# Prompt linear and softmax attention placed inside the paged attention of a hybrid decoder step

## The reference, cut to what matters

```
xn = rms_norm(h, norm1);  z = xn @ w_in                # q, k, v of both attentions, gates
S_t = diag(a_t) S_(t-1) + k_t^T v_t;  o_t = q_t S_t      # linear attention, 4 heads, in chunks
p   = softmax(q1 k1^T) - lam * softmax(q2 k2^T)          # differential softmax, 4 heads
o_diff(prompt) = p(causal, over meta + prompt) @ v
o_diff(sample) = p(over cache_k[page_table] and 4 new) @ [cache_v[page_table]; v_new]
h = h + [norm(o_gla) * silu(gate), norm(o_diff) * (1 - lam_init)] @ w_out
h = h + mixture_of_experts(rms_norm(h, norm2))           # top 1 of 4 groups, top 2 of 8 experts
```

## Time and profile before

| | us |
|---|---|
| median of 3 runs | 2400.14 (2399.14 to 2403.88) |
| the profiled execution | 2400.51 |
| its span, first to last instruction | 2398.7 |
| projection | 0 to 355 |
| linear attention, prompt | 355 to 509 |
| linear attention, samples | 509 to 548 |
| softmax attention, prompt | 548 to 778 |
| paged softmax attention | 778 to 1502 |
| merge and routing, experts, combine | 1502 to 2399 |

### The profile page before, as it was taken

How to read it: one execution, slowest core, us unless ns; L and a number is a source line. 1 busy time by engine, 2 the same in 40 slices (tenths; PEclk the granted TensorE clock), 3 DMA queues, 4 the chain that set the end, 5 groups by cost and what they waited for, 6 DMA issues and landing times. The chain is left out here.

```text
span 2398.7 us, 39482 instructions
## 1 busy us (share of the span) xinstructions
PE 2064.1 (86%) x14525; PEld 1516.4 (63%) x14525; DVE 1262.3 (53%) x1975; ACT 1083.9 (45%) x1919; POOL 406.0 (17%) x370
## 2 busy tenths in 40 slices
PE   6999998987887889889888888699179999999991
PEld 5777776765555566565565555255158888888870
DVE  4313414434665534533533533232478888888874
ACT  4312223312443434434434534322067777878760
POOL 0000000000000333233233232000212221212213
PEclk9999999975688999999999999799579999999995
DMA  5121115010000998998998998341079999999976
GB/s 176 49 76 53 64 51 205 1 27 13 1 1 10 392 406 350 404 371 361 392 381 365 380 392 312 133 176 44 10 288 385 404 405 405 404 403 399 407 296 234
DMA packets 106648, 577.14 MB, mean 241 GB/s; under 512 B 14592, under 2 KB 19840, under 8 KB 53520
## 3 DMA queue, kind: packets, MB, share of 16 engines
q0 software_dynamic: 44448, 293.89, 30.6%
q1 hardware_dynamic: 62064, 281.22, 30.3%
HBM read 531.26 MB, written 43.81 MB: 240 GB/s over the span
## 5 line engine op out<-in xcount | busy, mean ns | idle before, releaser
L1792 DVE TENSOR_TENSOR e_l<-first_w,e_h 128x1024 fp32r<-128x1024 f32 x256 | 294.7, 1218 | 10.1 <-ACT e_h L1789 9.9
L1189 PEld LDWEIGHTS ps<-ident,d_ring 128*128 128x128 f32 x2048 | 236.6, 148 | 97.1 <-ACT d_kT L1252 83.6
L1789 ACT CAST e_h<-first_w 128x1024 fp32r<-128x1024 f32 x256 | 250.3, 1049 | 82.3 <-POOLq L1861 42.7
L1252 ACT COPY d_kT<-ps 128x512 f32<-128x512 f32 x256 | 149.8, 586 | 274.7 <-PE ps L1189 272.2
L1189 PE MATMUL ps<-ident,d_ring 128*128 128x128 f32 x2048 | 263.4, 286 | 9.0 <-DMA d_ring<-in_cache_k,d_row 6.9
L1751 PE MATMUL ps<-e_h,e_xh 128*128 128x512 f32 x512 | 207.1, 404 | 3.6 <-DVE e_xl L1801 3.6
L1753 PE MATMUL ps<-e_h,e_xl 128*128 128x512 f32 x512 | 203.9, 398 | 0.0
L1752 PE MATMUL ps<-e_l,e_xh 128*128 128x512 f32 x512 | 203.9, 398 | 0.0
L1300 DVE COPY d_kT<-ps 128x512 f32<-128x512 f32 x256 | 172.4, 687 | 35.6 <-PE ps L1189 31.9
L1238 PE MATMUL ps<-d_ring,d_pT 128*8 128x128 f32 x4096 | 157.8, 280 | 18.2 <-issue 11.8
L304 PE MATMUL ps<-wh,xh 128*128 128x512 f32 (+1 forms) x432 | 173.4, 401 | 0.0
(11 more groups left out here) (321 smaller groups left out, 3513.5 us busy)
## 6 DMA issues: line engine op xcount, KB each, us to landing
first_w<-in_w_down SPq DMA_DIRECT2D x32, 2048.0 KB, 9.0
first_w<-in_w_up SPq DMA_DIRECT2D x62, 1024.0 KB, 8.8
first_w<-in_w_gate SPq DMA_DIRECT2D x62, 1024.0 KB, 11.3
ys_d<-e_y SPq DMA_DIRECT2D x32, 512.0 KB, 10.1
w<-in_w_in SPq DMA_DIRECT2D x6, 2048.0 KB
ys_d<-cat SPq DMA_DIRECT2D x1, 8192.0 KB, 24.7
kT<-in_x_prompt SPq DMA_DIRECT2D x8, 512.0 KB, 4.5
m_wout<-in_w_out SPq DMA_DIRECT2D x2, 2048.0 KB, 10.7
```

The costliest lines, as they stand in the source:

```text
L1189: mm = pe.transpose(k.ps[:, h, r * P:(r + 1) * P], ring[:, g % RING, r, h * P:(h + 1) * P], ident)
L1789: return act.copy(h13[:, :, kk, :], w13[:, :, kk, :])
L1792: return dve.tensor_tensor(l13[:, :, kk, :], w13[:, :, kk, :], h13[:, :, kk, :].bitcast(F32), ALU.subtract)
```

## The change

`linear_attention`, `sample_linear_attention`, `prompt_attention` and `sample_attention` become one function, `attention`, in one block without loops. The paged part is cut into 133 steps t of two halves each: a step turns the keys of group t in two times two heads, takes the scores of group t-1, and multiplies the probabilities of group t-4 with the values (`LAG = 4`). The loads alternate between a value group and a key group (`LOADS`), in a ring of 7 buffers. The prompt's work is cut into 171 phases; `schedule` puts one, in 18 cases an empty one, behind a half until they are used up, so that 171 phases lie over some 252 halves. All engines walk through the same list `SCHEDULE`.

The paged softmax keeps a running maximum: each chunk of two groups (1024 keys) has its exponentials against the maximum so far, and VectorE rescales the sum and the output (`update`). The probabilities are turned by a product with a 128x32 table `pick`, which takes the 8 rows of each head that hold queries, 8 products a chunk (`turn_probs`). The new keys come ahead of the loop, for all samples. The turned paged keys have two PSUM banks (0 for ScalarE, 1 for VectorE), scores bank 2, probabilities and outputs bank 3; the prompt's phases have banks 4 to 7.

Prompt softmax takes its maximum for each part of up to 512 keys and for the meta keys apart; `a_weights` and `a_combine` bring the parts to one scale when the head is done. `cat` no longer lies in SBUF during attention: outputs go to DRAM (`cat_d`) and the merge loads them tile by tile; it takes the sample rows last (`MERGED`). `qk` goes through DRAM too (`qk_d`). The fill of the spare rows moves into `project`.

```diff
+def prompt_phases():
+    order = [("h_decay", 0), ("rest", 0), ("h_turn", 0), ("h_pair", 0), ("h_out", 0), ("h_state", 0), ("rest", 0)]
+    for i in range(TILES):
+        order.append(("g_decay", i))
+        if i:
+            order += [("rest", i), ("rest", i)]
+        order.append(("g_state", i))
+        if i:
+            order += [("g_turn", i), ("g_pair", i), ("g_pair2", i), ("g_out", i)]
+    order.append(("values", 0))
+    for n in range(len(ATT) + 1):
...
+        for j in range(max(scores, outs)):
+            order.append(("a_step", (n, j)))
+def schedule():
+    phases, halves = prompt_phases(), 2 * (NT + LAG + 1)
+    order, done = [], 0
+    for x in range(halves):
+        order.append(("sample", (x // 2, x % 2)))
+        while done < len(phases) and done * (halves - 14) < len(phases) * (x + 1):
+            order.append(phases[done])
+            done += 1
+    return order + phases[done:]
...
+                # TensorE
+                def turn(t, h):
+                    if h == 0:
+                        arrived(pe, "k", t)
+                    if 2 * t + h // 2:
+                        pe.wait_ge(s_ktd if h % 2 else s_kta, 2 * t + h // 2)
+                    x = PLACE[("k", t)] % RING
+                    for r in range(GROUP):
+                        mm = pe.transpose(k.ps[:, h % 2, r * P:(r + 1) * P], ring[:, x, r, h * P:(h + 1) * P], ident)
+                def turn_probs(n):
...
+                    for g in range(2 * GROUP):
+                        mm = pe.matmul(k.ps[:, 3, 32 * g:32 * g + 32], s[:, n % 2, P * g:P * (g + 1)], pick, start=True, stop=True)
+                def sample(t, half):
+                    if half == 0:
+                        if t < NT:
+                            turn(t, 0)
+                            turn(t, 1)
+                        if 1 <= t <= NT:
+                            scores(t - 1)
+                        if t % 2 == 0 and 0 <= t - LAG < NT:
+                            turn_probs((t - LAG) // 2)
+                    else:
+                        if t < NT:
+                            turn(t, 2)
+                            turn(t, 3)
+                        if 0 <= t - LAG < NT:
+                            values(t - LAG)
+                def a_step(n, j):
+                    if n < len(ATT) and j < len(key_parts(ATT[n][0])):
+                        a_scores(n, j)
+                    if n:
+                        groups = len(turn_groups(ATT[n - 1][0]))
+                        if 1 <= j <= groups:
+                            a_values(n - 1, j - 1)
+                        if j < groups:
+                            a_turn(n - 1, j)
...
+                # ScalarE
+                def a_step(n, j):
+                    if n and j == 0:
+                        a_weights(n - 1)
+                    if n < len(ATT) and j < len(key_parts(ATT[n][0])):
+                        a_exponentials(n, j)
+                    if n:
...
+                            a_keep(n - 1, j)
...
+                # VectorE
+                def sample(t, half):
+                    n, odd = divmod(t - 2, 2)
+                    if half == 0:
+                        if not odd and 0 <= n - LAG // 2 < CHUNKS_N:
+                            update(n - LAG // 2)
+                        if t < NT:
+                            keep(t, 1)
+                        if not odd and 0 <= t - LAG < NT:
+                            keep_probs((t - LAG) // 2)
+                    else:
+                        if t < NT:
+                            keep(t, 3)
+                        if not odd and 0 <= n < CHUNKS_N:
+                            maximum(n)
+                def a_step(n, j):
+                    if n and j == 0:
+                        a_weights(n - 1)
+                        a_combine(n - 1)
+                    if n < len(ATT) and j < len(key_parts(ATT[n][0])):
+                        a_maxima(n, j)
```

1593 lines of the change are left out of this document (877 added, 716 removed).

## The result

The changed kernel takes 2444.53 us (2441.53 to 2449.25), the kernel before beside it 2399.64 (2393.85 to 2403.88): a ratio of 1.0191, interval 1.0163 to 1.0218. It is slower by 45 us where 22 us less were forecast. The time lies inside the range of 2290 to 2500, on the wrong side of the time before.

What follows compares the result with a forecast made beforehand. TensorE was to bound the stage, not the stream: 14 + 872 + 147 + 37 + 15 + 30 + 12 + 11 = 1138 us against 1160, so 2400.5 - 22 = 2378 us; range 2290 to 2500, likeliest case 2330 to 2430.

Steps and rivals of the forecast that it cites:

- What bounds the stage: Between projection and merge: TensorE becomes the bound, not the 640 us stream; stage about 1120 us, DMA share near 0.6.
- TensorE's work: At full clock: paged steps 611, linear attention 123, the samples' linear attention 18, prompt softmax 120; 872 us.
- the 36-column row: Routing matmul of the kernel before, 16 records in 1.87 us; used to price the table products at 0.9 a step.
- the prediction's four cases of the first wait: Waits for a_combine by slot, 2.4 to 3.9 us, occurring 11, 5, 10 and 6 times: mean 3.1, 96 us.
- The waits: TensorE waiting on other engines: prompt softmax 147 us, g_decay 37, the samples' linear attention 15.
- the copies behind `a_combine`: ScalarE's paged-key copies queued late: 2.1 us in empty slots, mean 1.1, 35 us; 13 for keys in two parts.
- The rival of ScalarE's late copies: Bank 0 uncopied after every first step, waits 3.5 us instead of 1.1: 74 us more, 2452 us; chance 0.13.
- The clock: Two thirds of 39 long TensorE waits drop it to 1.2 GHz, 1.2 us each: 30 us, bounds 0 and 100.
- The third rival: Long waits bring 5 us at half speed, 70 us; prompt blocks 1 to 3 another 60 to 70; 2480; chance 0.22.
- The rule of the skill: Cycling two PSUM banks instead of four would swing TensorE's clock between its levels, giving 2480 us.
- Start, end, projection: Around the stage: start 14 us, end 12, to the merge's first turn 11; projection's extra stores and fill nothing.
- The sign: Whole kernel: 22 us less than 2400.5; chances faster 0.50, the same 0.08, slower 0.42.

Runs made afterwards that it cites:

- half of the products: The changed kernel with half of the products with the table left out, four a chunk instead of eight: 2370.9 us, ratio 0.9892.
- the turns are moved: The changed kernel with a_turn and a_values one slot later than a_weights and a_combine: 2479.1 us, ratio 1.0373.
- the last kernel: The changed kernel with filled wait, split g_decay, four store buffers, earlier residual loads, dense list: 2336.0 us with 24 identity turns, 2342.5 us with 12.

## Why the prediction was wrong

*What bounds the stage.* Right. TensorE bounds it; the DMA share is 0.66, and a microsecond of work taken away gives a microsecond or more (half of the products). "A stage of about 1120 us" should have been 1170.5 from the first turn of keys.

*TensorE's work.* 892 us against 872, near enough. The products with the table are 1.97 us for 16 records by the row, 1.8 from start to start, as the 36-column row said. The step is 4.98 us where I had 4.8: turns 2.03 instead of 1.9 and values 1.05 instead of 1.0; times 128 this is 23 us, about the whole difference. (4.8 us times 128 is 614, where the sum has 611, and the prediction's four cases of the first wait make 32 where it has 31; neither changes anything.)

*The waits.* The mechanism was right and the places too. For `a_combine` I had 31 waits and 96 us, the trace has 31 and 90.7. At `g_decay` I had 37 us, and it has 31.8 (460 to 860 us). For the copies behind `a_combine` I had 48 us, and it has 8.9: ten of 31 such waits are not covered, about as the prediction had it, but they cost 0.9 us each and not 2.1. The rival of ScalarE's late copies is not what happened; it is what happens when the turns are moved (85.6 us).

*The clock.* This is the step that failed: "So short waits cost nothing, and two thirds of the 39 long ones drop the clock to 1.2 GHz for about 2.6 us of work, 1.2 us each: 30 us". It cost 122. Both factors were too small. Of the 39 long waits 34 have a fall, not 26, and such a fall takes 5.6 us in the mean and loses 2.4 us, where I took 2.6 and 1.2: 82 us instead of 30. I had priced a fall by one row of 3 us at 0.62 behind a wait of 2.27 and one of 4 us at 0.50 behind 6.55. The stretches behind those rows were not yet back at full clock:

```profile
970.00:974.00 4.00, 4.00 (x30) 4.00 (x29) 2.38 (x4) 1.76 (x3) 0.94 (x1) 0.76 1.01 416
...
1022.00:1025.00 3.00, 3.00 (x56) 2.06 (x52) 0.29 (x1) 3.00 (x10) 0.94 (x1) 0.81 0.21 30
```

With them the two falls had lost 2.2 and 1.7 us (busy time times the missing share of the clock), more than the 1.2 that I took. Another 21 us are a term that I put at nothing: the samples' linear attention, which the earlier trace rows shows at 0.50 before, stood in the sum at full clock ("I take 18"). Placed among the paged steps it has the clock at 0.50 for 45 us. The last 14 us are the meta scores and single falls (82 + 21 + 14 are the 117 of the finer count). The third rival, "the clock stays low", with 5 us at half speed behind every long wait, was nearest to the mechanism; it had 0.22, and its 2480 also had whole row blocks at half speed, which the trace does not show. With its first half alone, 70 us, the sum would have been 2448. That this is close to the 2444.5 measured is luck: the waits were 59 us too long in the sum, and the projection and the samples' part missing from it.

*The rule of the skill* (the Trainium skill, TensorE: Matmul & The Clock Gate, "A second HAM failure mode: psum-queue depth-cycling") tells of small idle gaps between groups of matmuls that cycle through banks, and of a clock that swings by them. I had taken from it that two banks alone would make the clock swing. They do not: with the same two banks and no long wait the paged steps stand at 1.00 for 630 us. The larger part of the swing is at `a_combine`; but the eight falls at `g_decay` stand at waits for one of the two banks, or for the running output, and whether four banks would have spared them no run shows.

*Start, end, projection.* The start took 21.5 us, since the products with all samples' new keys are strung out with their own waits (6.9 us for `d_q_pad`, then 3.4 of small ones); 7.5 us too little. The ends were 7 too much. "Nine more stores ... are both covered and cost nothing" was wrong by 15.6 us: I had compared shares of the DMA engines and not asked where in SP's queue the store stands and how many buffers ScalarE has ahead of it.

*The sign.* A gain of 22 us rested wholly on the clock term: the kernel before loses 102 us to the clock in this stretch, and the sum had 30. I had never counted the 102.

In all: work +20, clock +92, start +7.5, projection +15.6, waits -59, ends -7: some 69 us, where the profiled execution (2446.0 us) lies 68 over the forecast and the median 66.5.

## What to carry to other kernels

Count a wait of the bound engine twice: its length, and the work that follows at half clock. Follow the clock after the wait until it is back before giving it a price, and count what the kernel before loses to the clock in the same stretch. Where such a wait can't be removed, cheap work in it (turns of the identity into a bank that is free) bought 32 us here, and in the last kernel 12 turns did nearly as well as 24 (6.5 us apart). When phases are interleaved, try them dense as well as evenly spread: dense was 17 and 28 us faster here. And before a result that stayed in SBUF is sent to DRAM, look at how many buffers stand ahead of the queue that carries it.

## What the runs showed of the hardware that I had not expected

At 26 of 31 waits of 1.9 to 4.4 us the clock is at 1.2 GHz for 5.3 us in the mean. Waits of 1.4 us in the mean, 28 of them, leave it at 0.97 over 1055 us. Between these sizes the outcome is not fixed: the same 2.60 us had 0.79 behind it at one tile and 1.00 at another, and two waits of 2.6 and 1.5 us with 0.6 us of work between were followed by 0.50. The clock also falls without a wait, behind 16 records of 16 columns in four of eight cases, in six of eight with the waits filled. Turns alone, 24 in 2.84 us, keep the clock up. And one pass over the paged keys and values has TensorE at 97% and the stream at 407 GB/s together, so that it has next to no gap into which other work of TensorE would fit.
